# Half of an expert piece loaded ahead, bias tables moved to SyncE's queue, and later waits on TensorE, in a three-layer transformer kernel

## The chip, the cores and the metric

One core of a Trainium2 chip runs the whole program. The metric is the device time of one execution in microseconds. Three executions of the kernel before are known, and one profiled execution with its trace.

## The reference, cut to what matters

256 tokens of width 1024 go through three layers, all in float32. Layers one and two each have a mixer and then a retrieval step (PEER): every token picks 128 rows out of a table of 16384 (8 heads, 16 picks each), takes the dot product of its activation with the first half of the row, and adds the second half weighted by it. The third layer has a mixer with three kinds of attention, whose bias tables come from two small parameter tensors, and a mixture of 32 experts.

```
act = gelu(einsum('td,thkd->thk', xb, u[ib])) * gb      # retrieval, 128 tokens at a time
y   = einsum('thk,thkd->td', act, v[ib])
...
logits = einsum('bhcd,bhacjd->bhcaj', q_r, k_win) * scale + bias   # last mixer, one of its parts
...
a = silu(xb @ w1[e]) * (xb @ w3[e])                       # expert
return a @ w2[e]
```

## The kernel before, in words

Each engine has its own program, written out by hand; they meet in semaphores. SyncE (SP) issues nearly all loads of weights, GpSimd (POOL) the gathers, and each queue issues in program order: a wait stands in the way of everything behind it.

**Retrieval.** `PICKS` = 512 gathers, numbered 0 to 511, make up four tiles of 128 (two layers by two tiles of tokens). A gather (L1036) brings one picked row for each of 128 tokens, 8 KB each, so 1 MiB, into one of `ROWS` = 8 buffers. VectorE takes the dot product (L3153), ScalarE makes a diagonal matrix of the weights (`weigh_row`, L2305, L2308, L2311), and TensorE adds the row into PSUM (`sum_row`, L1560). POOL issues gather n only when gather n-8 has been summed. Between the rows the engines do the mixer of the next layer in small steps, by a step number s that is written out: `second_layer(t)` on TensorE (L1708) and on ScalarE. At s = 5, 64 and 81 TensorE transposes a tile of activations (`turn_tile`, L1632), ScalarE copies it into `hT` (`move_turned_tile`, L2366, L2371), and TensorE waits for the copy in the same step (`d_hT`), though the first product that reads it comes at s = 9, 67 and 84. `rows_to` is called at the top of every step, so sums that are due stand between the steps. This happens for both values of t: six places in all.

**The last mixer.** Its weights come in 10 slots of 2 MiB through a ring of `RING` = 4 places in the first 64 KB of `arena`, which the row buffers have used until then. SP waits for gather 509 (L870, `near`), and then loads the first four (L873), each when the row buffers in its place are summed: the first two need the sums of gathers 505 and 507, the third that of gather 510, the fourth that of gather 511. The fifth and later slots are loaded when TensorE has finished with the slot that had the place (L808). The bias tables, `dil_bias` (one transfer of 2304 KB in runs of 1536 bytes, L1040) and `na_bias` (16 transfers of 96 KB in runs of 256 bytes, L1045), are loaded by POOL once the last rows have been added to `x`, and then the gain `g_ffn` (512 KB, L956). VectorE adds a mask to `na_bias` in `mask_tables` (L2763) after the first two head scalings; the first reader of the tables is `last_bias(0)` (L2736).

**The experts.** They run in `QUADS` = 8 groups of four; a group has `PIECES` = 12 pieces of 2 MiB: 0 to 7 for `up` (L1967), 8 to 11 for `down` (L2016). Of group 0 the first `AHEAD` = 11 pieces are loaded before the stage, 0 to 7 in the eight `moe_slot` places (the last two of which are outside the ring) and 8 to 10 in leftover strips of other buffers (`BITS`). From piece 11 on all pieces go through `MOE_RING` = 6 places. TensorE counts pieces it has finished in `p_used`; SP waits for it before each load (`next_piece`, L882). Piece 11 takes the place of piece 0, and pieces 0 to 4 of group 1 those of pieces 1 to 5 of group 0; piece 5 of group 1 takes the place of piece 11, so it is issued at `p_used` = 12, after the whole `down(0)`.

Before the experts a router picks them. TensorE works out the router's products (`route_tile`, L1182), VectorE the choice (L3462 to L3504), and meanwhile TensorE transposes the scaled second tile of `h` (`turn_scaled`, L1201), ScalarE copies it to `hT` (`move_half`, L2472), and TensorE runs products whose results nobody reads (`keep_clock`, L1128). `hT` is read in the experts' stage only by a branch for experts with more than 32 tokens (L2044), which runs over all experts again when its flag is set.

Of the kernel before, what the change touches and what calls it, by code (L numbers as in the profile page):

```python
# [240 lines left out]
def program(nc, a, out):  # L241
    ctx = ExitStack()
    with ctx:
# [483 lines left out]

        def down_piece(q, n):
# [71 lines left out]
        def _(sync):  # L800
# [68 lines left out]
            near = PICKS - 3  # L869
            sync.wait_ge(row_in[near % ROWS], landed(near))  # L870
            for n in range(phase_slots["in2"][0], phase_slots["in2"][0] + RING):
                sync.wait_ge(vsum, rows_left(place[n]))
                sync.dma_start(ring[:, place[n], :], a["w_slots"][n]).then_inc(w_landed[place[n]], 16)  # L873
            for n in range(phase_slots["in2"][0] + RING, len(slots)):
# [28 lines left out]
            sync.wait_ge(r_mm, T)  # L903
            sync.wait_ge(y_ready, 3)
# [39 lines left out]
        def _(pool):  # L944
# [74 lines left out]
            for n in range(PICKS):  # L1019
# [13 lines left out]
                else:  # L1033
# [5 lines left out]

            pool.dma_start(dil_bias, bass.AP(tensor=t5_rep.tensor, offset=127,  # L1040
                                             ap=[[12 * TW - 1, P], [TW, 12], [1, 384]])).then_inc(bias_in, 16)
            W = NA_HEADS * NDR * RW
            for hh in range(NA_HEADS):
                for r2 in range(2):
                    pool.dma_start(na_bias[r2 * GRID_W:(r2 + 1) * GRID_W, hh, :].rearrange("p (j n) -> p j n", j=6),  # L1045
                                   bass.AP(tensor=na_rep.tensor,
                                           offset=hh * NDR * RW + (1 - r2) * RW + GRID_W - 1,
                                           ap=[[W - 1, GRID_W], [RW, 6], [1, GRID_W]])).then_inc(bias_in, 16)
# [11 lines left out]
        def _(pe):  # L1060
# [135 lines left out]
            def turn_scaled(b):  # L1196

                n = turned[0]
                for c in range(4):
                    k = 4 * b + c  # L1200
                    mm = pe.transpose(sp_[:, b, c * P:(c + 1) * P], h[:, 1, k * P:(k + 1) * P], ident)  # L1201
# [2471 lines left out]
```

## Time and profile before

| | us |
|---|---|
| median of 3 executions | 2306.08 (2305.84 to 2307.43) |
| the profiled execution | 2306.09 |
| its span in the trace | 2304.3 |
| TensorE busy | 1789.9 (78%) |
| VectorE busy | 1298.3 (56%) |
| ScalarE busy | 850.6 (37%) |
| GpSimd busy | 659.1 (29%) |
| moved by DMA | 920.49 MB, 399 GB/s over the span |

Times in the trace count from the span's start. A busy share is an average over stages with different limits; what bounds a stage is read in the stage.

### The profile page before, as it was taken

The numbers are of one execution on the slowest core, as the hardware profiler recorded it, in microseconds if no ns is written. First come the engines' busy times: TensorE is split into PE (matmuls) and PEld (weight loads), VectorE is DVE, ScalarE is ACT, GpSimd is POOL, SyncE is SP. The second block draws the span as 40 slices with busy tenths as digits, with TensorE's granted clock in tenths as the row PEclk, the third lists the DMA queues.
The fourth block names the chain that finished last, engine by engine and source line by source line (L and its number), as shares of the span: only waits on it lengthen the run. The fifth ranks groups of instructions, "written<-read, shape, count | busy, mean of one in ns | idle before, by whom it ended". The sixth has DMA issues, their size and how long they took to land.

```text
span 2304.3 us, 30881 instructions
## 1 busy us (share of the span) xinstructions
PE 1789.9 (78%) x11196; PEld 848.4 (37%) x11196; DVE 1298.3 (56%) x3217; ACT 850.6 (37%) x2292; POOL 659.1 (29%) x606
## 2 busy tenths in 40 slices
PE   9999877695797777588779666877779997766666
PEld 4655521161352343153336112343327553222222
DVE  4878887668757766866776867555442331111111
ACT  1324354444445544454744435444333520000000
POOL 1002444434433433533443444333322300000000
PEclk9999887696798888689989667888979999788888
DMA  9988799999999999999999999999999399999998
GB/s 395 381 351 347 314 420 421 420 420 419 388 421 421 421 421 421 421 382 421 412 410 421 421 420 421 421 421 420 421 404 333 121 392 422 428 428 429 428 428 372
DMA packets 111150, 920.49 MB, mean 399 GB/s; under 512 B 12806, under 2 KB 15140, under 8 KB 19044
## 3 DMA queue, kind: packets, MB, share of 16 engines
q0 software_dynamic: 76800, 549.70, 57.9%
q1 hardware_dynamic: 34212, 369.02, 38.8%
q8 instruction: 78, 1.28, 0.2%
q14 instruction: 60, 0.49, 0.1%
HBM read 917.57 MB, written 6.06 MB: 401 GB/s over the span
## 4 chain that ended last, share of the span: by engine, by line
DMA 48%; PE 32%; DVE 10%; ACT 6%; issue 3%; POOL 1%; SPq 0%; DVEq 0%; POOLq 0%; ACTq 0%
DMA arena<-in_peer_uv_dram,arena 27%; DMA arena<-in_moe_pieces_dram 14%; PE summed L1560 8%; DVE y_g L3153 4%; PE gp L1652 3%; PE gp L1105 3%; DMA mod<-in_w_parts_dram 3%; DMA arena<-in_w_slots_dram 2%; PE gp L1967 2%; PE gp L1110 2%; PE gp L1648 2%; DMA arena<-in_w_parts_dram 1%; PE gp L1781 1%; ACT arena L2311 1%; PE gp L1532 1%
## 5 line engine op out<-in xcount | busy, mean ns | idle before, releaser
L1560 PE MATMUL summed<-arena 64*64 64x512 f32 x4096 | 693.8, 773 | 338.5 <-ACT arena L2311 313.9
L3153 DVE CUSTOM_DVE_ANT_0 y_g<-arena,h 128x1024 f32<-128x1024 f32 x512 | 627.3, 1225 | 389.6 <-DMA arena<-in_peer_uv_dram,arena 332.1
L1036 POOL DMA_INDIRECT arena<-in_peer_uv_dram,arena x512 | 592.8, 1158 | 885.9 <-PE summed L1560 805.4
L1560 PEld LDWEIGHTS summed<-arena 64*64 64x64 f32 x4096 | 136.3, 157 | 760.3 <-ACT arena L2311 660.3
L2305 ACT ACTIVATE arena<-arena 128x1 f32<-128x1 f32 x512 | 102.7, 201 | 558.0 <-DVE arena L3153 556.9
L1967 PE MATMUL gp<-arena,mod 128*32 128x512 f32 x1008 | 156.5, 758 | 98.5 <-DMA arena<-in_moe_pieces_dram 98.5
L2311 ACT ACTIVATE arena<-cst,arena 128x128 f32<-128x128 f32 x512 | 205.5, 401 | 16.8
L3546 DVE TENSOR_TENSOR mod<-mod,gp 128x512 f32<-128x512 f32 x8 | 5.5, 687 | 353.7 <-ACT mod L2620 353.7
L2308 ACT ACTIVATE arena<-arena 128x1 f32<-128x1 f32 x512 | 150.8, 294 | 16.6
L1967 PEld LDWEIGHTS gp<-arena,mod 128*32 128x32 f32 x1008 | 31.7, 124 | 214.8 <-DMA arena<-in_moe_pieces_dram 156.8
L2620 ACT ACTIVATE mod<-gp 128x512 f32<-128x512 f32 x8 | 4.8, 597 | 246.7 <-PE gp L1967 246.7
L1105 PE MATMUL gp<-arena,hT 128*128 128x512 f32 x208 | 92.8, 603 | 1.0 <-DMA arena<-in_w_slots_dram 0.5
L2884 DVE SCALAR_TENSOR_TENSOR h<-arena,cst,h 128x512 f32<-128x512 f32 x98 | 73.9, 754 | 3.4
L2305 ACT ACT_TABLE_LOAD x54 | 69.3, 1283 | 0.9
L1942 PE MATMUL summed<-mod,h 128*128 128x128 f32 x256 | 46.8, 368 | 22.5 <-DVE mod L3541 22.4
L3065 DVE FIND_INDEX8 arena<-arena 128x8 uint32<-128x128 f32 (+1 forms) x192 | 61.7, 329 | 0.0
L3062 DVE MAX8 arena<-arena 128x8 f32<-128x128 f32 (+1 forms) x192 | 58.4, 332 | 5.6 <-ACT arena L2280 2.2
L1105 PEld LDWEIGHTS gp<-arena,hT 128*128 128x128 f32 x208 | 39.5, 194 | 52.5 <-issue 50.1
L2093 ACT ACTIVATE arena<-gp 128x512 f32<-128x512 f32 (+1 forms) x26 | 15.3, 589 | 113.6 <-PE gp L1119 40.3
L1119 PE MATMUL gp<-hT,arena 128*128 128x256 f32 x256 | 56.3, 381 | 0.7 <-ACT hT L2105 0.7
L2016 PE MATMUL scores<-arena,mod 128*32 128x256 f32 x952 | 54.3, 380 | 0.7 <-ACT mod L2624 0.7
L1942 PEld LDWEIGHTS summed<-mod,h 128*128 128x128 f32 x256 | 45.3, 279 | 25.0 <-DVE mod L3541 24.0
(530 smaller groups left out, 2339.3 us busy)
## 6 DMA issues: line engine op xcount, KB each, us to landing
arena<-in_moe_pieces_dram SPq DMA_DIRECT2D x92, 2048.0 KB, 25.5
arena<-in_w_slots_dram SPq DMA_DIRECT2D x43, 2048.0 KB, 12.5
arena<-in_w_parts_dram SPq DMA_DIRECT2D x42, 1024.0 KB, 9.3
mod<-in_w_parts_dram SPq DMA_DIRECT2D x23, 1024.0 KB, 9.6
arena<-in_peer_uv_dram,arena POOLq DMA_INDIRECT x512, 15.7
t_rep<-t_rows POOLq DMA_DIRECT2D x1, 3066.0 KB, 18.3
arena<-t_rep POOLq DMA_DIRECT2D x1, 2304.0 KB, 12.8
ext<-in_w_parts_dram SPq DMA_DIRECT2D x2, 1024.0 KB, 22.8
```

Source lines behind the costliest of these rows:

```text
L1036: pool.indirect_dma_start(rowbuf[b], None, a["peer_uv"].rearrange("l n d -> (l n) d"), bass.IndirectOffsetOnAxis(ap=idx[:, col(n):col(n) + ...
L1105: mm = pe.matmul(bank, hT[:, k, grp[1] * P:(grp[1] + 1) * P], w[:, k, :], start=k == 0, stop=k == KT - 1)
L1560: mm = pe.matmul(op[o:o + HALF, b, :], diag[i:i + HALF, n % DIAGS, i:i + HALF], rowbuf[n % ROWS][i:i + HALF, D + b * 512:D + (b + 1) * 512 ...
L1652: mm = pe.matmul(bank[:, c * P:(c + 1) * P], w[k][:, c * P:(c + 1) * P], hT[:, k, tok], start=k == 0, stop=k == KT - 1)
L1942: mm = pe.matmul(op[:, k // 4, (k % 4) * P:(k % 4 + 1) * P], h[:, t, k * P:(k + 1) * P], sel[:, t, :], start=t == 0, stop=t == T - 1)
L1967: mm = pe.matmul(gp[c, j, :], xe[:, 2 * kk + k, c], w[:, e, k, :], start=kk + k == 0, stop=kk == 3 and k == 1, skip_group_check=True)
L2305: link(act.activation(coef[:, c:c + 1], dots[:, c:c + 1], ACT.Gelu))
L2308: link(act.activation(coef[:, c:c + 1], coef[:, c:c + 1], ACT.Copy, scale=gate[:, c:c + 1]))
L2311: act.activation(diag[:, n % DIAGS, :], ident, ACT.Copy, scale=coef[:, c:c + 1]).then_inc(diag_ready, 1)
L2884: ins = v.scalar_tensor_tensor(out=acc, in0=w[:, k, :], scalar=cact[:, k:k + 1], in1=acc, op0=ALU.mult, op1=ALU.add)
L3065: ins = v.max_index(w[:, part], b[:, part], s)
L3153: v.tensor_tensor_reduce(y[:, t, :], rowbuf[n % ROWS][:, 0:D], h[:, t, :], 1.0, 0.0, ALU.mult, ALU.add, dots[:, c:c + 1]).then_inc(udot, 1)
```

## The change

1. TensorE's waits for `d_hT` after `turn_tile` move from the steps s = 5, 64 and 81 to 9, 67 and 84 (both t).
2. The bias tables are loaded by SP, behind the last mixer's first four weight slots and ahead of its fifth, on the semaphore `loaded`. The wait for `bias_w` and for the two halves of `x` comes with them. POOL goes from the last gather to the gain and `divide_last`.
3. Of the first four slots only the first is still issued behind gather 509; the second waits for gather 511 to land.
4. `mask_tables` comes first in VectorE's `last_attention`.
5. A square root on one column (`small[:, 16:17]`, written by ScalarE and read by nobody) is inserted behind the last row on ScalarE.
6. `turn_scaled` and `move_half` of the router's stage move into the rarely taken branch, there for both tiles. So `hT` is free from the router's products on.
7. The first half of piece 11 of group 0 (1 MiB) is loaded into `hT`, behind the router's products (`r_mm`) and ahead of the last two strips of pieces 9 and 10. At `p_used` = 1 only the second half is left to load, into the ring's place. The strips' semaphore counts one more transfer, and TensorE waits for it before it reads piece 11.

```diff
@@ down_piece
+            if isinstance(q, int) and q == 0 and n == AHEAD:
+                split = [flat_hT[:, c:c + S] for c in range(0, 8 * S, S)]
+                split += [moe_slot[piece_place(q, n)][:, c:c + S] for c in range(8 * S, 16 * S, S)]
+                return lambda e, f: split[4 * e + f]
@@ piece_landed
-                return 16 if n not in BITS else 16 * sum(len(bits) for bits in BITS.values())
+                return 16 if n not in BITS else 16 * (1 + sum(len(bits) for bits in BITS.values()))
@@ SyncE
-            near = PICKS - 3
-            sync.wait_ge(row_in[near % ROWS], landed(near))
             for n in range(phase_slots["in2"][0], phase_slots["in2"][0] + RING):
+                if n < phase_slots["in2"][0] + 2:
+                    near = PICKS - 3 if n == phase_slots["in2"][0] else PICKS - 1
+                    sync.wait_ge(row_in[near % ROWS], landed(near))
                 sync.wait_ge(vsum, rows_left(place[n]))
                 sync.dma_start(ring[:, place[n], :], a["w_slots"][n]).then_inc(w_landed[place[n]], 16)
+            sync.wait_ge(bias_w, 64)
+            sync.wait_ge(x_ready, 4 * T + 1)
+            sync.dma_start(dil_bias, bass.AP(...)).then_inc(loaded, 16)
+            for hh in range(NA_HEADS):
+                for r2 in range(2):
+                    sync.dma_start(na_bias[...], bass.AP(...)).then_inc(loaded, 16)
...
             sync.wait_ge(r_mm, T)
+            sync.dma_start(flat_hT, a["moe_pieces"][0, AHEAD][:, 0:8 * S]).then_inc(p_in[AHEAD - 1], 16)
             sync.wait_ge(y_ready, 3)
             sync.wait_ge(h_ready, 5 * T + 5)
             first_bits(9, (1, 2))
             first_bits(10, (1, 2))
             for n in range(AHEAD, PIECES):
                 sync.wait_ge(p_used, n - AHEAD + 1)
-                next_piece(0, n)
+                r = piece_place(0, n)
+                sync.dma_start(moe_slot[r][:, 8 * S:], a["moe_pieces"][0, n][:, 8 * S:]).then_inc(p_in[r], 16)
@@ GpSimd
-            pool.dma_start(dil_bias, ...).then_inc(bias_in, 16)
-            for hh in range(NA_HEADS):
-                for r2 in range(2):
-                    pool.dma_start(na_bias[...], ...).then_inc(bias_in, 16)
@@ TensorE, second_layer (the same at s == 64 / 67 and 81 / 84)
                     if s == 5:
                         pe.wait_ge(d_h, 2 * t + 1)
                         turn_tile(h, t)
+                    if s == 9:
                         pe.wait_ge(d_hT, 6 * t + 2)
@@ TensorE, router
             pe.wait_ge(h_ready, 5 * T + 7)
-            turn_scaled(0)
-            turn_scaled(1)
             keep_clock("out2", 2, h[:, 0, 0:CH])
@@ TensorE, down
                     pe.wait_ge(p_in[r], piece_landed(p, 8 + b))
+                    if first(p) and 8 + b == AHEAD:
+                        pe.wait_ge(p_in[AHEAD - 1], piece_landed(p, AHEAD - 1))
@@ TensorE and ScalarE, in the branch on the flag
+                for t in range(T):
+                    for b in range(2):
+                        turn_scaled(t, b)      # ScalarE: move_half(b, (gp, sp_)[t][:, b, :], t)
@@ ScalarE
             rows_to(PICKS)
+            act.activation(small[:, 16:17], eps[:, 0:1], ACT.Sqrt)
             half_square(1, 0, x_ready, 4 * T)
...
-            act.wait_ge(r_mm, T)
-            for b in range(2):
-                move_half(b, sp_[:, b, :])
@@ VectorE
-                v.wait_ge(bias_in, 16 * (NA_HEADS + 17))
+                v.wait_ge(loaded, 16 * (NLOADS + 20))
...
             def last_attention():
+                mask_tables()
                 head_inverse("block2", 0)
                 head_scale("block2", 0)
                 head_scale("block2", 1)
                 head_inverse("block2", 1)
-                mask_tables()
```

## Rows read from the trace of the kernel before

**Rows 1.** The page: rates in 40 slices, and the chain that ended last, by engine.
```profile
GB/s 395 381 351 347 314 420 421 420 420 419 388 421 421 421 421 421 421 382 421 412 410 421 421 420 421 421 421 420 421 404 333 121 392 422 428 428 429 428 428 372
DMA 48%; PE 32%; DVE 10%; ACT 6%; issue 3%; POOL 1%; SPq 0%; DVEq 0%; POOLq 0%; ACTq 0%
```

**Rows 2.** Busy time by stretch: stretch, length, engines, granted clock, DMA share, GB/s.
```profile
615.00:619.00 4.00, 4.00 (x32) 1.08 (x24) 2.99 (x9) 2.31 (x8) 2.23 (x2) 0.70 0.37 111
640.00:960.00 320.00, 244.89 (x1545) 116.43 (x1547) 225.81 (x571) 158.01 (x441) 130.82 (x108) 0.84 1.01 421
991.00:995.00 4.00, 4.00 (x24) 1.24 (x20) 2.77 (x9) 2.50 (x10) 2.19 (x2) 0.50 0.51 166
1167.00:1170.00 3.00, 3.00 (x22) 1.96 (x15) 2.75 (x7) 0.85 (x3) 2.39 (x3) 1.00 0.79 265
```

**Rows 3.** Timeline of TensorE: start, duration, engine, line, work, [idle before <- releaser].
```profile
609.91 1.97 PE L1632 MATMUL turned<-cst,h 128*128 128x128 f32 x8
614.01 5.32 PE L1560 MATMUL summed<-arena 64*64 64x512 f32 x32 [2.13 <-ACT hT L2371]
990.22 6.65 PE L1560 MATMUL summed<-arena 64*64 64x512 f32 x32 [2.14 <-ACT hT L2371]
1163.50 4.49 PE L1560 MATMUL summed<-arena 64*64 64x512 f32 x24 [1.43 <-ACT hT L2366]
```

**Rows 4.** Timeline of GpSimd, the gather behind the first of these places.
```profile
616.29 1.48 POOL L1036 DMA_INDIRECT arena<-in_peer_uv_dram,arena  x1 [4.94 <-PE summed L1560]
```

**Rows 5.** Timeline of ScalarE at the same place.
```profile
609.76 0.40 ACT L2311 ACTIVATE arena<-cst,arena 128x128 f32<-128x128 f32 x1
611.06 2.90 ACT L2371 ACTIVATE hT<-turned,cst 128x128 f32<-128x128 f32 x8 [0.89 <-PE turned L1632]
```

**Rows 6.** Timeline at the last gathers: SyncE's issues, and VectorE's last two rows.
```profile
1701.77 0.81 SPq L873 DMA_DIRECT2D arena<-in_w_slots_dram  x2
1704.24 1.23 DVE L3153 CUSTOM_DVE_ANT_0 y_g<-arena,h 128x1024 f32<-128x1024 f32 x1 [1.23 <-DMA arena<-in_peer_uv_dram,arena]
1709.16 1.23 DVE L3153 CUSTOM_DVE_ANT_0 y_g<-arena,h 128x1024 f32<-128x1024 f32 x1 [3.69 <-DMA arena<-in_peer_uv_dram,arena]
```

**Rows 7.** The last mixer's start: timelines, line L1045, and a stretch with tables.
```profile
1713.36 8.67 PE L1105 MATMUL gp<-arena,hT 128*128 128x512 f32 x16
1717.70 1.28 ACT L2479 ACT_TABLE_LOAD   x1
1731.14 0.33 SPq L808 DMA_DIRECT2D arena<-in_w_slots_dram  x1
1738.00:1740.00 2.00, 2.00 (x21) 2.00 (x20) 0.00 (x0) 1.32 (x3) 0.00 (x0) 1.00 0.94 198
1745.90 2.28 PE L1110 MATMUL gp<-hT,arena 128*128 128x128 f32 x18
L1045 POOL DMA_DIRECT2D mod<-na_rep x16: 662/669/745, 1718.6 to 1757.2; - x16
1766.53 3.84 DVE L2763 TENSOR_TENSOR mod<-mod,cst 128x384 f32<-128x384 f32 x8 [2.33 <-DMA mod<-na_rep]
```

**Rows 8.** Timeline of the router's stage, TensorE and VectorE.
```profile
1863.22 1.96 PE L1201 MATMUL scores<-cst,h 128*128 128x128 f32 x8
1867.09 0.29 DVE L3496 TENSOR_TENSOR arena<-arena 128x32 f32<-128x32 f32 x2
1867.54 0.31 PE L1927 MATMUL turned<-arena,mod 128*128 128x32 f32 x2
```

**Rows 9.** The experts' start: SyncE's issues before and after its long wait; DMA there.
```profile
1875.24 2.04 SPq L882 DMA_DIRECT2D arena<-in_moe_pieces_dram  x2
1883.83 0.33 SPq L882 DMA_DIRECT2D arena<-in_moe_pieces_dram  x1
1905.47 0.33 SPq L882 DMA_DIRECT2D arena<-in_moe_pieces_dram  x1
1905.00:1908.00 3.00, 3.00 (x36) 1.04 (x32) 0.00 (x0) 1.02 (x1) 0.00 (x0) 1.00 0.89 300
```

More of the change, by code:

```diff
@@ L726, in program @@
         moe_slot = [ring[:, place[n], :] for n in last_held] + [zbuf[:, 0:4096], tk[:, 0:4096], arena[:, 28672:32768], y_g2[:, :]]
+        flat_hT = hT[:, :, :].rearrange("p k n -> p (k n)")
         def down_piece(q, n):
@@ L867, in _ @@
                 sync.dma_start(ring2[q % 2], a["w_parts"][WQ1 + PARTS + 2 + i]).then_inc(w1_in[q % 2], 16)
-            near = PICKS - 3
-            sync.wait_ge(row_in[near % ROWS], landed(near))
             for n in range(phase_slots["in2"][0], phase_slots["in2"][0] + RING):
+                if n < phase_slots["in2"][0] + 2:
+                    near = PICKS - 3 if n == phase_slots["in2"][0] else PICKS - 1
+                    sync.wait_ge(row_in[near % ROWS], landed(near))
                 sync.wait_ge(vsum, rows_left(place[n]))
                 sync.dma_start(ring[:, place[n], :], a["w_slots"][n]).then_inc(w_landed[place[n]], 16)
+            sync.wait_ge(bias_w, 64)
+            sync.wait_ge(x_ready, 4 * T + 1)
+            sync.dma_start(dil_bias, bass.AP(tensor=t5_rep.tensor, offset=127,
+                                             ap=[[12 * TW - 1, P], [TW, 12], [1, 384]])).then_inc(loaded, 16)
+            W = NA_HEADS * NDR * RW
+            for hh in range(NA_HEADS):
+                for r2 in range(2):
+                    sync.dma_start(na_bias[r2 * GRID_W:(r2 + 1) * GRID_W, hh, :].rearrange("p (j n) -> p j n", j=6),
+                                   bass.AP(tensor=na_rep.tensor,
+                                           offset=hh * NDR * RW + (1 - r2) * RW + GRID_W - 1,
+                                           ap=[[W - 1, GRID_W], [RW, 6], [1, GRID_W]])).then_inc(loaded, 16)
             for n in range(phase_slots["in2"][0] + RING, len(slots)):
@@ L1038, in _ @@
             pool.wait_ge(x_ready, 4 * T + 1)
-            pool.dma_start(dil_bias, bass.AP(tensor=t5_rep.tensor, offset=127,
-                                             ap=[[12 * TW - 1, P], [TW, 12], [1, 384]])).then_inc(bias_in, 16)
-            W = NA_HEADS * NDR * RW
-            for hh in range(NA_HEADS):
-                for r2 in range(2):
[L1045 to L1048, printed above, removed]
             load_gain(5, a["g_ffn_2"][0])
@@ L1194, in turn_plain, with turn_scaled @@
                 turned[0] += 1
-            def turn_scaled(b):
+            def turn_scaled(t, b):
                 n = turned[0]
@@ L1738, in second_layer @@
                         turn_tile(y, t)
+                    if s == 67:
                         pe.wait_ge(d_hT, 6 * t + 4)
@@ L1744, in second_layer @@
                         turn_tile(h, t)
+                    if s == 84:
                         pe.wait_ge(d_hT, 6 * t + 6)
@@ L2467, in half_square, with move_half @@
                                accum_out=small[:, 46 + b:47 + b]).then_inc(sumsq, 1)
-            def move_half(b, bank):
+            def move_half(b, bank, t=1):
                 act.wait_ge(turn_done, turned[0] + 1)
-                act.activation(hT[:, 4 * b:4 * b + 4, P:S], bank.rearrange("p (c n) -> p c n", c=4), ACT.Copy).then_inc(turn_moved, 1)
+                act.activation(hT[:, 4 * b:4 * b + 4, t * P:(t + 1) * P], bank.rearrange("p (c n) -> p c n", c=4), ACT.Copy).then_inc(turn_moved, 1)
                 turned[0] += 1
@@ L2657, in _ @@
             with act.If(act.value_load(flag[0:1, 0:1], min_val=0, max_val=2 * S) > 0):
+                for t in range(T):
+                    for b in range(2):
+                        move_half(b, (gp, sp_)[t][:, b, :], t)
                 expert(0, 0)
```

2 lines of the change are left out of this document (1 added, 1 removed).

## The prediction, made before the changed kernel was run

> **What bounds the kernel now.** I read the page's rates first [rows 1]. From slice 6 on most slices stand at 420 to 429 GB/s, and a slice is 57.6 us. The retrieval steps (about 240 to 1710 us) and the experts (from about 1875 us) are bound by transfers. The chain of waits gives DMA 48% and TensorE 32%; TensorE's share lies mostly in the last mixer, the slices at 333 and 121 GB/s, where its products run back to back.
>
> The next view is the busy time by stretch. The long stretch 640 to 960 us shows the full rate, 421 GB/s at a DMA share of 1.01 [rows 2]. A change inside a stretch like that gains nothing by freeing an engine. So I looked for places where the rate falls, and found three short ones: 615 to 619 us at 111 GB/s, 991 to 995 at 166, 1167 to 1170 at 265 [rows 2]. Against 421 they lose 4 x (1 - 111/421) = 2.9 us, 2.4 us and 1.1 us.
>
> **The waits on TensorE (part 1).** TensorE's timeline shows what comes before each dip [rows 3]. At 609.91 it transposes for 1.97 us, then stands idle for 2.13 us until ScalarE's copy L2371 ends, and only then sums at 614.01. Yet ScalarE had finished the diagonals of the two gathers that were due by 610.16, before its 2.90 us of copies began [rows 5]. POOL waits for these sums before it issues the next gather, which comes at 616.29 after 4.94 us of waiting [rows 4]. From 615 on there is nothing in flight. The second place is the same with 2.14 us of idle time, the third has 1.43 us [rows 3].
>
> With the wait moved to the step that reads `hT`, the sums start 2.13 us sooner, the two later ones of the four are ready by then, and step 9 finds the copy long done. Gather 140 is issued 2.1 us sooner. The dip is longer than that (2.9 us), so the whole 2.1 us comes back, and the stage runs at full rate afterwards, which keeps it. The terms are 2.1 us, 2.1 us (dip 2.4), and 1.1 us at the third, where the dip is shorter than the stall. At the other three of the six places the rate never falls, so there the gain is nothing: those rows are covered by gathers in flight. Sum: **-5.3 us**. Bounds: nothing, if TensorE's later steps take it up; the three dips together, 6.4 us.
>
> **The second weight slot held back (part 3).** The last two gathers were taken up at 1704.24 and 1709.16, 4.92 us apart [rows 6], where full rate gives 1 MiB in 2.49 us. So the weight slots issued at 1701.77 cost the last gather some 2.4 us. The change leaves the first slot where it is and takes away only the second. The first alone holds 2 MiB, 4.98 us of all engines, and until 1709 that much more than covers what was mixed in. I take **0**: the last gather still has a weight transfer beside it to the end. The bound on the other side is the whole 2.4 us. The Trainium skill, "DMA: Bandwidth & Descriptors", section "Queues, rings and completion order", says that each DMA engine takes turns between queues packet by packet. By that rule one slot in SP's queue costs the gather as much as two, which agrees with my 0; sharing by transfers in flight would give back a third of the 2.4 us, 0.8 us.
>
> **The square root ahead (part 5).** It takes the table load of 1.28 us at 1717.70 off the path of the norm. But TensorE's L1105 runs from 1713.36 to 1722.03 and must end before the next step [rows 7], so this gains **0**; if L1105 did not cover it, 1.28 us.
>
> **The tables on SP's queue (parts 2 and 4).** On POOL the 16 transfers of `na_bias` were issued from 1718.6 to 1757.2, and the mask ran at 1766.53 in its place [rows 7]. TensorE was busy through all of that, so earlier tables give nothing. The cost is the fifth weight slot, now behind them in one queue. It was issued at 1731.14, and TensorE needs it at 1745.90 [rows 7]. I work out when it lands. The second slot is issued at 1709.2; with some 1.5 us until bytes flow (an estimate, from the dip that ends about that long after POOL's issue at 616.29), three slots of 4.90 us at the page's 428 GB/s end at 1725.4. `dil_bias` (2.36 MB) takes 5.5 us, the gain on POOL's queue, now earlier, 1.2 us. For `na_bias` (1.57 MB) the nearest row is the stretch 1738 to 1740, filled mostly with it, at 198 GB/s: 7.9 us. Then 4.9 us for the slot: 1744.9. That is 1.0 us before the need: **0**. By bytes alone it is 4.2 us earlier. The upper bound is POOL's own pace, 38.6/15 = 2.6 us for each table. Everything behind the waiting SP is this slot and the later ones, whose needs lie 7 us apart.
>
> A rule speaks against this part. The same page, section "Issuing engines are not separate DMA queues", says that starting transfers from several engines saves only time to issue them. By it the move costs no bandwidth and buys none.
>
> **The router's stage (part 6).** Eight transposes of 1.96 us go. The products behind them wait for VectorE's choice, which ends at 1867.38, and L1927 starts at 1867.54 [rows 8]. At most 0.1 us comes forward. ScalarE's two copies are beside the path too. I take **0**.
>
> **Half a piece ahead (part 7).** 1 MiB less in a stage bound by transfers looks like 2.45 us. But the ring is fed by TensorE here. SP issued the ring's first piece at 1875.24, its sixth at 1883.83 and nothing more until 1905.47, when `down(0)` was done and the place of piece 11 came free [rows 9]. In between the queue lived on six pieces, 6 x 4.90 = 29.4 us: with the 1.5 us to the first byte it was dry at 1906.1, and the next piece's bytes came at 1907.0. The stretch 1905 to 1908 agrees, 300 GB/s instead of 428, a loss of 0.9 us. With half a piece less it runs dry 2.4 us earlier, and piece 5 of group 1 is still issued when `down(0)` ends. The dip grows by what was saved. The half in `hT` and the strips behind it are needed only in `down(0)`, after `up(0)` and a gather, so their 2.4 us of delay is covered; without that cover it would be paid. So **0**; the other bound is 2.45 us.
>
> **Sum.** The profiled execution took 2306.09 us (span 2304.3 and 1.8 around it), within 0.01 of the median. 2306.1 - 5.3 = **2300.8 us**, span 2299.0. Some 0.2%, 4.6 us, is about what a measurement of this kernel can tell from no change; the bounds are 2301.5 and 2310.7.
>
> **The rivals.**
> *A: the tables delay the fifth slot a little.* If a table takes 0.6 to 0.9 us on SP's queue instead of 0.49 (runs of 256 bytes; the stretch that I priced was not all tables), the slot lands up to 5.5 us late: 2301.5 to 2306. For it: the margin is only 1 us.
> *B: the earlier sums come to nothing.* TensorE has 32 products of L1652 per pair of rows after step 9; if these pace the stage, the gathers are still late afterwards and 1 to 3 us of the 5.3 remain: 2303 to 2305. Against it: TensorE's whole schedule moves by the same 2.1 us.
> *C: more than I allow.* The last gather lands on time (2.4), or the half piece pays (2.45), the reading that a transfer-bound stage pays by bytes: about 2298.4, or 2296 with both. Against it: rows 6 and 9.
> *D, slower: the tables hold SP.* If SP is held for each table as POOL was, 2.6 us each, it reaches the fifth slot at 1718 + 17 x 2.6 = 1762, which lands about 6.4 us later, 22 us after the need: 2323. It decides from 0.49 + 6.3/16 = 0.88 us per table on, where margin (1.0) and gain (5.3) are used up; at 1.2 us it is slower by over 0.2%. Against it: POOL's pace is that of its issues, while the stretch above shows tables moving five times as fast.
> *E: the change does not do what it says*: the half piece ahead is such a part, and it is in the forecast.
>
> **How the numbers follow.** Forecast 0.52 (its own range 2299.3 to 2302.3, a fifth of it above 2301.5), A 0.20, B 0.12, C 0.10, D 0.06. Faster by over 0.2%: 0.42 of the forecast and all of C, 0.52. Slower: D and what lies beyond A, 0.07. Within: 0.41. The range runs from 2298.0, in the middle of C, to 2306.5, the end of A; it leaves out D and half of C.
>
> **What would show it.** Right: no idle time of TensorE on L2371 or L2366 before L1560; 615 to 619 near full rate, and everything behind it 2 us earlier; the last gather still some 4.9 us after the one before; TensorE never idle on the fifth slot; a deeper dip ahead of the issue at `p_used` = 12. Wrong: dips that stay though the waits are gone (B), TensorE waiting for a weight slot near 1745 (A or D), or a stage from 1905 on that is shorter than before (C).

## The result: slower by 0.35%, and the profile after

| | us |
|---|---|
| kernel before, median of 7 runs | 2307.1 (2305.8 to 2310.8) |
| changed kernel, median of 7 runs | 2314.84 (2312.95 to 2316.85) |
| ratio, 95% interval | 1.0035 (1.0025 to 1.0045) |
| profiled execution, span | 2312.7 (before 2304.3) |

I had forecast 2300.8 us. The changed kernel is about 8 us slower than the one before, outside my range. The spans of the two profiled executions differ by 8.4 us. First the stretches of [rows 2] again, in the changed kernel: stretch, length, engines, granted clock, DMA share, GB/s.

```profile
615.00:619.00 4.00, 3.19 (x27) 1.74 (x28) 2.67 (x10) 3.17 (x11) 2.73 (x2) 1.00 1.02 401
640.00:960.00 320.00, 245.98 (x1534) 115.30 (x1526) 225.97 (x570) 158.10 (x441) 137.59 (x108) 0.83 1.01 420
991.00:995.00 4.00, 4.00 (x37) 1.97 (x30) 2.56 (x10) 2.96 (x11) 3.08 (x4) 1.00 0.83 297
1167.00:1170.00 3.00, 3.00 (x15) 2.64 (x15) 2.86 (x8) 1.72 (x6) 1.77 (x2) 1.00 0.96 355
```

The dips filled, the first wholly and the other two in large part: 401 GB/s instead of 111, 297 instead of 166, 355 instead of 265. But the stage did not get shorter. VectorE's sum over a tile's rows (L3172, now L3189), the last step of a tile, starts at 597.05 before and 597.98 after for the first tile, and at 1713.50 and 1714.49 for the last. That is 1116.45 us in one and 1116.51 in the other. The 0.9 us at 597 lies ahead of all that was changed there.

Then the last mixer. The timelines of SyncE's queue and TensorE, and two stretches (lines moved: L808 is now L814, L1110 is L1121). The last two rows are the same stretches in the kernel before:

```profile
1718.40 25.29 SPq L889 DMA_DIRECT2D mod<-na_rep  x16
1743.73 32.81 SPq L814 DMA_DIRECT2D arena<-in_w_slots_dram  x6
1751.62 16.18 PE L1121 MATMUL gp<-hT,arena 128*128 128x128 f32 x128 [4.48 <-DMA arena<-in_w_slots_dram]
1734.00:1738.00 4.00, 4.00 (x38) 4.00 (x37) 0.00 (x0) 0.00 (x0) 0.00 (x0) 1.00 1.02 178
1738.00:1742.00 4.00, 4.00 (x38) 4.00 (x38) 0.00 (x0) 1.32 (x3) 0.00 (x0) 1.00 0.75 140
```
```profile
1734.00:1738.00 4.00, 4.00 (x39) 4.00 (x38) 0.00 (x0) 0.00 (x0) 2.53 (x4) 1.00 1.01 404
1738.00:1742.00 4.00, 4.00 (x39) 4.00 (x37) 0.00 (x0) 1.32 (x3) 0.00 (x0) 1.00 1.02 260
```

SyncE needs 25.29 us to hand over 16 tables. It issues the fifth weight slot at 1743.73 instead of 1731.14 [rows 7], and TensorE stands idle for 4.48 us until it has landed. The products behind the wait, 128 of them, take 16.18 us, at a granted clock of 0.58 from 1751.6 to 1754; in executions without a wait they take 14.56. From the start of L1105 to the start of VectorE's choice (L3496) the stretch has grown from 153.73 to 160.09 us: **+6.4**.

And the router's stage, TensorE's timeline and its granted clock:

```profile
1874.79 0.61 PE L1939 MATMUL turned<-arena,mod 128*128 128x32 f32 x2 [2.24 <-DVE arena L3513]
1874.00:1876.00 2.00, 1.21 (x6) 1.21 (x7) 1.23 (x9) 0.00 (x0) 0.00 (x0) 0.71 1.02 438
1876.00:1878.00 2.00, 2.00 (x5) 0.92 (x5) 1.49 (x7) 0.00 (x0) 0.00 (x0) 0.50 1.00 422
1878.00:1880.00 2.00, 2.00 (x11) 2.00 (x10) 1.79 (x8) 0.00 (x0) 0.00 (x0) 0.50 0.91 385
```

TensorE has nothing to do for 2.24 us, and behind the choice its granted clock is 0.5 (1.2 GHz): the work that took 0.31 us in [rows 8] takes 0.61 now. From the choice to the start of `down(0)` it is 33.12 us instead of 31.20: **+1.9**. From there to the end it is 405.1 instead of 406.0: **-0.9**. With the 1.0 us that was there at L1105 (0.9 of it at 597) this adds up to 8.4.

### The profile page after: what moved, and what is told of

It is laid out like the page before. It is cut to its first block, busy times and chain, and to the rows that moved or that the text cites. A ratio compares the mean times of both kernels' runs of the same rounds, so it can differ in the third digit from the quotient of the medians.

```text
span 2312.7 us, 30863 instructions
## 1 busy us (share of the span) xinstructions
PE 1788.8 (77%) x11188; PEld 848.1 (37%) x11188; DVE 1297.3 (56%) x3217; ACT 851.2 (37%) x2291; POOL 652.9 (28%) x589
## 4 chain that ended last, share of the span: by engine, by line
DMA 46%; PE 34%; DVE 9%; ACT 6%; issue 3%; SPq 1%; POOL 1%; DVEq 0%; POOLq 0%; ACTq 0%
DMA arena<-in_peer_uv_dram,arena 26%; DMA arena<-in_moe_pieces_dram 14%; PE summed L1571 8%; DVE y_g L3170 4%; PE gp L1663 3%; PE gp L1116 3%; PE gp L1130 2%; PE gp L1979 2%; DMA arena<-in_w_parts_dram 2%; DMA mod<-in_w_parts_dram 2%; PE gp L1795 1%; PE gp L1659 1%; ACT arena L2328 1%; SPq L889 1%; PE gp L1543 1%
## 5 line engine op out<-in xcount | busy, mean ns | idle before, releaser
L1979 PEld LDWEIGHTS gp<-arena,mod 128*32 128x32 f32 x1008 | 31.6, 124 | 215.5 <-DMA arena<-in_moe_pieces_dram 157.7
L1954 PEld LDWEIGHTS summed<-mod,h 128*128 128x128 f32 x256 | 45.2, 278 | 25.2 <-DVE mod L3558 24.1
```

The costliest lines, as they stand in the source:

```text
L1954: mm = pe.matmul(op[:, k // 4, (k % 4) * P:(k % 4 + 1) * P], h[:, t, k * P:(k + 1) * P], sel[:, t, :], start=t == 0, stop=t == T - 1)
L1979: mm = pe.matmul(gp[c, j, :], xe[:, 2 * kk + k, c], w[:, e, k, :], start=kk + k == 0, stop=kk == 3 and k == 1, skip_group_check=True)
```

## Experiments

Every kernel was timed against the one before on the same chip. Their intervals are 2 to 4 us to each side, so for single microseconds I read the traces. Four stretches serve for that, each from start to start: the stage of the rows (first to last L3172), the mixer (L1105 to L3496), from there to `down(0)` (L2016), and the rest. Of each kernel there is one profiled execution, which need not lie at the median.

### Each part alone

`waits_only` is the kernel before with part 1:

```
                         turn_tile(h, t)
+                    if s == 9:
                         pe.wait_ge(d_hT, 6 * t + 2)
```

> The kernel before with part 1 alone (the waits for the copies of hT moved to the steps that read it). The forecast's theory: the 2.1, 2.1 and 1.1 us that TensorE stood still are gained, 5.3 us. The rival, from the trace of the changed kernel (its third tile of gathered rows ends 0.99 us later than before, as its first tile did already, whose code is the same): the time is given back further on in the same stage, where stretches of 420 us and more a slice now stand lower: 0, within 1 us. In both the idle time of TensorE on L2371 is gone and 615 to 619 us stands near 400 GB/s; what differs is the end of the last tile of rows, about 1708 or about 1713.5.

Measured: 0.9991 (0.9981 to 1.0002). The stretch 615 to 619 stood at 395 GB/s, and 619 to 623, where the same work lies in this execution, which is 4.3 us later at the first tile, at 389. The stage took 1116.95 us. The forecast's 5.3 us are not there.

`tables_sp` has parts 2 and 4, `dil_bias` and the 16 tables moved from POOL's program to SP's:

```
+                    sync.dma_start(na_bias[r2 * GRID_W:(r2 + 1) * GRID_W, hh, :]..., ...).then_inc(loaded, 16)
...
+                mask_tables()
                 head_inverse("block2", 0)
```

> The kernel before with parts 2 and 4 alone (the bias tables on SyncE's queue, their mask earlier; the second weight slot is not held back). Theory T: a table costs 0.65 us on SP's queue, 16 of them 10.4 us, dil_bias 6.4, and the fifth weight slot lands behind them. The queue is not dry for 2.5 us as it was in the changed kernel at 1708 to 1711, so the slot lands about 2.5 us earlier than its 1751.6 less 1: near 1748, 2 us after the need of 1745.9, and TensorE's clock, which fell after the wait, costs up to 1.7 us more: +2 to +4 us. The forecast's theory: 0, TensorE never waits for the fifth slot. Rival: the cost in the changed kernel came from the tables alone, slot held back or not: +6.4 us.

Measured: 1.0024 (1.0015 to 1.0033), +5.5 us. Its mixer took 159.48 us instead of 153.73, +5.75.

```profile
1717.07 24.71 SPq L882 DMA_DIRECT2D mod<-na_rep  x16
1741.82 32.79 SPq L808 DMA_DIRECT2D arena<-in_w_slots_dram  x6
1749.68 16.18 PE L1112 MATMUL gp<-hT,arena 128*128 128x128 f32 x128 [4.26 <-DMA arena<-in_w_slots_dram]
```

So the tables alone make most of the loss, and more than the +2 to +4 that I expected, although the queue was not dry here.

`router_only` has part 6:

```
             pe.wait_ge(h_ready, 5 * T + 7)
-            turn_scaled(0)
-            turn_scaled(1)
             keep_clock("out2", 2, h[:, 0, 0:CH])
```

> The kernel before with part 6 alone (the eight transposes of h and the two copies of hT's second half are done only in the branch that hardly runs). Theory C: with the transposes gone TensorE runs out of work some 2 us before VectorE's choice is there, its granted clock falls to 0.5, and what stands behind it takes 3 us longer, of which 1 us is given back in the gathers: +2 us, with the granted clock at 0.5 to 0.7 in the 4 us behind the choice. The forecast's theory: 0. Rival: the 2 us of the changed kernel came from the half piece and the strips behind it; then this is 0 though the clock falls.

Measured: 1.0000 (0.9989 to 1.0011). Choice to `down(0)`: 31.26 us, as before. Here the clock fell too, but from 1866 to 1870, under the filling products ahead of the choice, and had come back (0.96 in 1870 to 1872). The loss is thus not part 6 as such. It comes when the low clock falls behind the choice.

That happens without part 6 too. In `tables_half` and `dil_on_sp` (both below), which keep the transposes, TensorE stood idle for 1.40 us ahead of the choice's result, and then its clock was low. Both rows are from `tables_half`:

```profile
1870.86 0.41 PE L1937 MATMUL turned<-arena,mod 128*128 128x32 f32 x2 [1.40 <-DVE arena L3507]
1872.00:1874.00 2.00, 2.00 (x6) 1.07 (x5) 1.86 (x9) 0.00 (x0) 0.00 (x0) 0.50 0.95 404
```

Over all sixteen profiled kernels: where TensorE idled 2.2 us there, the clock was low behind the choice in four of four; where it idled 1.4 us, in two of eight; where it idled 0.5 us or not at all, in none of four. In the kernel before, the clock was low ahead of the choice (0.58 from 1865 to 1867), which stretched the products until the choice was there. In the six executions with the low clock behind it the stretch from the choice to `down(0)` took 32.4 to 33.1 us, in the ten others 30.0 to 31.6. `tables_half` and `dil_on_sp`, at 32.65 and 32.87 us, have neither part 6 nor the half piece, so the growth needs neither.

`all_but_tables` is the changed kernel without parts 2 and 4:

> The changed kernel with parts 2 and 4 undone (the tables back on POOL's queue, their mask in its old place). Theory T: the 6.4 us that the stretch from the last gathered row to the end of the fifth slot's groups grew by are gone: about 2308.4 us, +1 to +2 against the kernel before. Rival: the slot held back is what makes the fifth slot late; then TensorE still waits for it near 1746 us, and 3 to 4 us remain there: 2311 to 2312.

Measured: 1.0001 (0.9991 to 1.0011). The mixer took 154.31 us and TensorE did not wait for the fifth slot. Its clock was low behind the choice, and from there to `down(0)` it took 32.95 us. What is left of the change is worth nothing, in sum.

### What about the tables costs

`tables_slot_held` adds part 3 to `tables_sp`:

```
+                if n < phase_slots["in2"][0] + 2:
+                    near = PICKS - 3 if n == phase_slots["in2"][0] else PICKS - 1
+                    sync.wait_ge(row_in[near % ROWS], landed(near))
```

> The kernel before with parts 2, 3 and 4 (tables on SyncE's queue and the second weight slot held back until the last gathered row has landed). Theory T+G: the tables cost the 5.5 us of the run with them alone; the slot held back leaves the queues dry near 1708 to 1711 us, 2.3 us of transfers that then lie ahead of the tables and the fifth slot, which TensorE gets near 1751.5 us: +7.5 to +8 us against the kernel before, +2.3 against the run with the tables alone. Rival: held back or not, the fifth slot is late by the tables only: +5.5. The forecast's theory: 0.

Measured: 1.0037 (1.0024 to 1.0051). The time fits either theory, the trace (of the fastest of its five executions, 2311.87 us) doesn't: the transfers did run thin, 238 GB/s at 1710 to 1714, but the mixer took 159.64 us, TensorE waited 3.97 us, and SyncE was through with the tables at 1742.99, 28.6 us after the start of L1105, just as in `tables_sp` (28.8). The slot held back costs nothing that shows beside the tables, and the +2.3 us that I had expected for it is not there: SyncE sets the time of the fifth slot, not the bytes ahead of it.

`tables_half` leaves 8 of the 16 tables on POOL's queue:

```
             for hh in range(NA_HEADS):
-                for r2 in range(2):
+                for r2 in range(1):
                     sync.dma_start(na_bias[r2 * GRID_W:(r2 + 1) * GRID_W, hh, :]...
```

> The kernel before with dil_bias and only 8 of the 16 tables on SP's queue; the other 8 stay on POOL's, and the mask stays in its old place. Theory T (a price for each table, 0.65 us on SP's queue): 8 x 0.65 = 5.2 us less ahead of the fifth slot, which in the run with all 16 held TensorE up for 4.26 us: no wait, 0 against the kernel before, within 1 us. Rival Q: what makes the slot late is its place behind three slots and dil_bias in one queue, the tables for POOL take the same bytes from the same engines: TensorE still waits 2 to 3 us for the fifth slot, +3 us or more.

Measured: 1.0037 (1.0023 to 1.0051). The profiled execution is the fastest of its five, 2311.0 us against a median of 2314.25; what the other four lost beyond it no trace shows.

```profile
1717.92 23.26 SPq L882 DMA_DIRECT2D mod<-na_rep  x8
1741.23 31.40 SPq L808 DMA_DIRECT2D arena<-in_w_slots_dram  x6
1749.33 14.56 PE L1120 MATMUL gp<-hT,arena 128*128 128x128 f32 x128 [2.27 <-DMA arena<-in_w_slots_dram]
```

Half the tables hold SyncE for 23.26 us instead of 24.71. So the time is not one price times the number of tables, and theory T, which had no wait here, falls. The single issues say more. With all 16 tables, in the changed kernel, the first lasted 9.69 us, the next five 1.5 to 2.0 us each, and the last ten 0.63 us each, one of them 0.93. With 8 the first lasted 10.86 us and the fourth 4.12. The longest and the shortest stand in the view of the line (shortest/median/longest, in ns), here the changed kernel and then `tables_half`:

```profile
L889 SPq DMA_DIRECT2D mod<-na_rep x16: 626/634/9687, 1718.4 to 1742.8; - x16
L882 SPq DMA_DIRECT2D mod<-na_rep x8: 625/1564/10862, 1717.9 to 1740.6; - x8
```

I read this as SyncE standing in the first issues while the weight slots and `dil_bias` ahead are moved; only the last ten of 16 go at the 0.65 us that theory T gave to all.

`dil_on_sp` leaves all 16 tables on POOL's queue and moves `dil_bias` alone:

```
+            sync.dma_start(dil_bias, ...).then_inc(loaded, 16)
...
-            pool.dma_start(dil_bias, ...).then_inc(bias_in, 16)
```

> The kernel before with dil_bias alone on SP's queue; all 16 tables of na_bias stay on POOL's, and the mask stays in its place. Idle time of TensorE on the fifth weight slot was 4.26 us with 16 tables on SP's queue and 2.27 us with 8. Theory P (each table on SP's queue costs the slot 0.25 us and more, as small packets that the same copy on POOL's queue does not have): with none of them the line through both ends at 0.3 us: no wait or a trace of one, 0 against the kernel before, and up to 1 us faster where POOL's tables, now started earlier, spare VectorE its wait ahead of the mask. Rival Q (being ahead of the slot in time is what counts, whatever queue it comes by): TensorE still waits 2 us or more for the slot, +2 us or more.

Measured: 1.0009 (1.0001 to 1.0018), about +2 us. That is what rival Q had, but not for its reason: SyncE issued the fifth slot at 1732.83, when its place came free, and TensorE did not wait for it. The mixer took 154.93 us, 1.2 more than before, and 1.7 us more went by behind the choice, at the low clock. POOL issued its last table at 1763.58 (before 1757.2, in an execution that was 1.8 us earlier at L1105), VectorE waited 5.29 us ahead of the mask, and TensorE 1.21 us behind that:

```profile
1771.17 3.84 DVE L2767 TENSOR_TENSOR mod<-mod,cst 128x384 f32<-128x384 f32 x8 [5.29 <-DMA mod<-na_rep]
1775.97 1.14 PE L1259 MATMUL scores<-arena 64*128 64x256 f32 x8 [1.21 <-DVE arena L2727]
```

This wait is there in the kernel before too [rows 7, the last]; in its profiled execution TensorE's other work covered it.

Two kernels then held another engine, or held SyncE one slot later. `tables_half_scalar` issues the 8 tables of `tables_half` on ScalarE's own queue, ahead of `last_projection()` in its program:

```
             move_turned_rows(1)
+            for hh in range(NA_HEADS):
+                act.dma_start(na_bias[0:GRID_W, hh, :]..., ...).then_inc(loaded, 16)
             last_projection()
```

> As the run with 8 tables and dil_bias on SP's queue, with these 8 tables on ScalarE's queue instead, issued in its gap behind the copies of hT (1723.6 to 1731.1). Theory H (SyncE is held: in the run with 8 tables it reached the fifth slot at 1741.2 instead of 1731.1, and TensorE waited 2.27 us): SyncE issues the slot as in the kernel before, within 1 us of the place being free, and TensorE does not wait for it; 0 to +1 us against the kernel before, from the small packets and from VectorE's wait ahead of the mask. Rival Z (the small packets' engine time ahead of the slot is what counts): TensorE still waits 1.5 to 2.5 us for the slot though it was issued in time. A third outcome, that ScalarE is held by its own queue past 1731, would show as TensorE idle on ScalarE's copy of the first groups.

Measured: 1.0051 (1.0034 to 1.0067), +11.8 us, and it is the third outcome. Timelines of ScalarE's queue, ScalarE, SyncE's queue and TensorE:

```profile
1724.44 23.45 ACTq L2585 DMA_DIRECT2D mod<-na_rep  x7
1747.93 0.60 ACT L2096 ACTIVATE arena<-gp 128x512 f32<-128x512 f32 x1 [23.50 <-issue]
1731.92 50.83 SPq L808 DMA_DIRECT2D arena<-in_w_slots_dram  x6
1748.67 10.28 PE L1113 MATMUL gp<-hT,arena 128*128 128x128 f32 x64 [9.64 <-ACT arena L2096]
```

SyncE is free and issues the slot in time (the 50.83 us are six slots with waits between). ScalarE is held instead, for 24.1 us by 8 tables, with nothing ahead of them in its own queue. What moved in 1715 to 1765 us, in this kernel and in the one before (queue, kind: packets, MB, share of the 16 engines):

```profile
q1 hardware_dynamic: 2228, 12.35, 69.9%
q10 hardware_dynamic: 3200, 0.79, 9.5%
q0 software_dynamic: 528, 1.31, 8.8%
```
```profile
q1 hardware_dynamic: 864, 12.57, 68.9%
q0 software_dynamic: 1295, 3.93, 27.4%
```

In q10 are the 8 tables, 0.79 MB in 3200 packets, 400 for a table of 96 KB. In the kernel before all 16 tables and `dil_bias`, 3.93 MB, went in 1295 packets of POOL's queue. An estimate from the shares: q10 used 9.5% of 50 us, 4.75 us, 0.6 us of engine time for a table; yet the 8 took five times as long, beside `dil_bias` and weight slots in SyncE's queue (q1). The first three issues on ScalarE took 0.64 to 0.69 us each, the seventh 10.83. The Trainium skill, "DMA: Bandwidth & Descriptors", section "Queues, rings and completion order", says that a DMA engine changes between queues after a packet; small packets that take turns with large ones would be held up like this. The trace agrees with that: from 1729 to 1746 us q1 moved 1447 packets and q10 1709, near to one for one, but 4.86 MB and 0.42 MB. No run here took the large ones away.

`slot_then_tables` issues the fifth slot first, and then `dil_bias` and all 16 tables:

```
+            load_weights(phase_slots["in2"][0] + RING)
             sync.wait_ge(bias_w, 64)
```

> As the run with all tables on SP's queue, with the fifth weight slot issued ahead of dil_bias and the 16 tables. SyncE waits for the slot's place until 1731 us and only then hands the tables over. Theory H: the fifth slot is on time, and the hold moves to the sixth, which is issued after 1731 + 0.4 + 16 x 0.63 = 1741.5 at the earliest, up to 1750 if the ring holds SyncE as it did; it lands 7 to 8 us later, against a need at 1753.2: a wait of 0 to 4 us, and the mask, whose tables now land near 1750, is not late. Against the kernel before: 0 to +4 us, and less than the +5.5 us of the run with the tables first. Rival Z: the same bytes and packets lie ahead of the sixth slot, +4 to +6 us.

Measured: 1.0046 (1.0030 to 1.0062), +10.6 us.

```profile
1730.16 20.56 SPq L883 DMA_DIRECT2D mod<-na_rep  x16
1750.77 26.07 SPq L808 DMA_DIRECT2D arena<-in_w_slots_dram  x5
1759.29 8.80 PE L1113 MATMUL gp<-hT,arena 128*128 128x128 f32 x64 [7.80 <-DMA arena<-in_w_slots_dram]
```

The hold moves with the tables, and the sixth slot pays. The time lies beyond both forecasts, H's 0 to +4 us and Z's +4 to +6; what speaks for H is that the sixth slot was late in its issue. I had allowed an issue by 1750; it came at 1750.77 and the slot landed 8.5 us later. The need was at 1751.5, not 1753.2, as this execution reached L1105 1.6 us earlier. Theory H names the mechanism, my price was too low.

### Where the 5.3 us went

`transposes_doubled` does the opposite of part 1, each transpose at the six places twice:

```
-                    for c in range(4):
+                    for c in range(8):
+                        c = c % 4
```

> The kernel before with each transpose at the six places of part 1 done twice, so that TensorE and the copies behind it are 2 us later at each, the opposite of part 1. The forecast's theory (a dip of the transfers at three of the six places costs the stage what TensorE is late): the stage from the end of the first tile of rows (597.05) to the end of the last (1713.50), 1116.4 us, grows by 2 us at each of the three dips or more, +6 us. Rival B (the stage has slack elsewhere that takes up what is won or lost at these places): it grows by 0 to 2 us.

Measured: 1.0001 (0.9985 to 1.0017). The sums behind the first place began 5.23 us after the start of the transposes, against 4.10 in [rows 3]. That is 1.1 us more, not 2, as the wait for ScalarE's copy became shorter, 1.59 us instead of 2.13. At the other two dips it is 0.9 and 1.0 us, so the forecast's theory would give +3 us here and not +6. The stage took 1116.27 us. Over all profiled kernels it took 1116.16 us on average in the five with part 1 (1115.41 to 1116.95) and 1116.5 in the ten that have neither part 1 nor the doubled transposes (1114.91 to 1118.13): a difference of 0.4, inside the spread of either. So the stage takes up what is won or lost at these places.

Two things can be ahead, and they part here: the transfers and the rows. On average over the five kernels with part 1 and the ten without, each counted from the end of its first tile, the gathers 140 to 168 (615 to 701 us) are issued 1.8 to 2.6 us sooner, and the bytes moved are ahead by 2.3 us of full rate. But gathers 172 to 198 (712 to 787 us) are issued only 0.4 us sooner, and VectorE takes up its rows only 0.2 us sooner (rows 140 to 171) and then 0.5 us (rows 172 to 198). The second tile ends 376.09 us after the first instead of 376.40, the third 752.82 instead of 753.25. Behind the second dip it is the same: gathers 272 to 296 are issued about 3 us sooner, gather 300 (1089 us) 0.1. In the kernel before and in `waits_and_dil` (below), which has part 1, the second and third tile end at:

```profile
973.25 0.68 DVE L3172 TENSOR_TENSOR y_g<-y_g,summed 128x512 f32<-128x512 f32 x1
1350.27 0.68 DVE L3172 TENSOR_TENSOR y_g<-y_g,summed 128x512 f32<-128x512 f32 x1
```
```profile
973.76 0.68 DVE L3179 TENSOR_TENSOR y_g<-y_g,summed 128x512 f32<-128x512 f32 x1
1350.69 0.68 DVE L3179 TENSOR_TENSOR y_g<-y_g,summed 128x512 f32<-128x512 f32 x1
```

The first tile ended at 597.05 and 597.61. So hardly any of the first 2.1 us ever reached VectorE's rows, and the gathers had lost most of it by 712 us. Which engine held them back is not shown.

The lead of the transfers lasts longer, and the trace shows where it goes. It is the stretch 1110 to 1160 us, in which VectorE has both the dot products and the attention's work. The kernel before, then `waits_and_dil`: the stretch, and all that VectorE waited for in it (waited for: us in total, times, longest):

```profile
1110.00:1160.00 50.00, 36.20 (x255) 15.48 (x253) 42.80 (x100) 35.81 (x96) 22.62 (x19) 0.90 1.01 412
DVE h L3218 <- PE scores L1679: 2.1, 1, 2.1
DVE arena L3218 <- PE scores L1679: 1.3, 1, 1.3
DVE den L3230 <- PE gp L1704: 1.3, 1, 1.3
DVE small L3274 <- ACT small L2447: 0.2, 1, 0.2
```
```profile
1110.00:1160.00 50.00, 36.16 (x252) 15.34 (x252) 42.73 (x101) 35.82 (x96) 22.25 (x19) 0.89 0.98 377
DVE h L3225 <- PE scores L1682: 2.2, 1, 2.2
DVE arena L3225 <- PE scores L1682: 1.3, 1, 1.3
DVE den L3237 <- PE gp L1707: 1.3, 1, 1.3
DVE small L3281 <- ACT small L2453: 0.2, 1, 0.2
```

VectorE does the same 42.8 us of work and waits for no gathered row, in either. The engines set the pace here, and rows that came earlier only thin the transfers out: 377 GB/s instead of 412, which over 50 us is 50 x (412 - 377)/421 = 4.2 us of transfers, an estimate (the busy share of the DMA engines fell less, from 1.01 to 0.98). In the five kernels with part 1 the rate was 377 to 393 here, 385 on average, in the ten without it 395 to 420, 408 on average: 50 x (408 - 385)/421 = 2.7 us. A second place is 760 to 780 us, 388 to 419 GB/s with part 1 and 412 to 421 without. I did not try a kernel that makes VectorE faster in these stretches, so where the lead goes is read from the traces, not shown by a run.

### The half piece, and the clock

`router_half_piece` has parts 6 and 7, `router_half_piece_clock` has three more filling products ahead of the choice:

```
-            keep_clock("out2", 2, h[:, 0, 0:CH])
+            keep_clock("out2", 5, h[:, 0, 0:CH])
```

> The kernel before with parts 6 and 7 (transposes only in the branch, half of piece 11 ahead into hT). In the changed kernel the stretch from VectorE's choice to down(0) grew by 1.9 us and what is behind down(0) shrank by 0.9. Theory R (the ring is pinned by down(0)): the half piece alone brings nothing before down(0) and its strips cost nothing; all of the growth is TensorE's clock at 0.5 behind the choice. So: about +1 us where the clock falls there, 0 or -0.5 where it doesn't. Rival S: the strips behind the half piece are late for down(0) or share the queues with the first gathers: +1 to +2 us in this stretch at full clock too.

> As the run before it, with five instead of two filling products ahead of the choice, so that TensorE has work until the choice is there (the three added take up to 3 us at full clock, 5 us at half). Theory R: the clock stays at 1.00 or has come back by the choice, the stretch from the choice to down(0) is 31.3 us as in the kernel before, and what is behind it is 0.5 to 0.9 us shorter: -0.5 to -1 us. Rival S: still 32 to 33 us. Should the added products run past the choice, they hold the rank's products up by 1 to 2 us, which the timeline would show.

Measured: 0.9996 (0.9987 to 1.0005) and 1.0007 (0.9997 to 1.0017). Choice to `down(0)` took 32.76 us in the first, where the clock was 0.50 in 1870 to 1872, and 31.57 in the second, where it stayed at 1.00. So theory R holds there: the growth is the clock, 1.2 us of it. But the -0.5 to -1 us that I had forecast for the second is not there. The added products ran past the choice by some 0.2 us, and the profiled execution had a wait of 3.75 us of TensorE behind the mask, whose tables were late on POOL's queue; whether the other executions lost the gain in the same way no trace shows. Behind `down(0)` the five kernels with the half piece took 405.8 us on average (405.1 to 406.4), the eleven others, the one before among them, 406.3 (405.7 to 407.8): by these averages, whose ranges overlap, the half piece is worth some 0.5 us, not its 2.45.

### Candidates

`waits_and_dil` has part 1 and `dil_bias` on SP's queue, `waits_dil_half_piece` parts 6 and 7 as well:

> A candidate for the best version: the kernel before with part 1 and with dil_bias alone on SP's queue. The sum of the two runs with each alone: part 1 gave a ratio of 0.9991, dil_bias 0 to -1 us by theory P: 2304 to 2307 us, -1 to -3 against the kernel before. By rival Q of the first run here: +0 to +2.

> The run before it with parts 6 and 7 as well, which alone gave a ratio of 0.9996: behind down(0) 0.6 to 0.9 us shorter, ahead of it up to 1.6 us longer where TensorE's clock falls behind the choice. Against the run before it: -0.5 to +1 us. If the half piece paid by its bytes (2.45 us), it would be 2 us faster.

Measured: 1.0004 (0.9995 to 1.0012) and 1.0006 (0.9997 to 1.0014). TensorE waited 0.19 and 0.27 us for the fifth slot and about 1.5 us behind the mask. Neither is faster than the kernel before, and no version here is faster by more than the measurement can tell.

## Why the prediction was wrong

**The waits (part 1): the step "the whole 2.1 us comes back, and the stage runs at full rate afterwards, which keeps it" failed.** The dips were read right, and filled. But I took a gather issued sooner for a row taken up sooner. VectorE took up the rows behind the first dip 0.2 to 0.5 us sooner, not 2.1, and by the end of the second tile 0.3 us were left, although the rate in 640 to 960 was full before and after. What the transfers were still ahead went in 1110 to 1160, where the engines set the pace. Rival B came true whole, not in part; whether by the products of TensorE that it names is open. Measured: 0.4 us of the 5.3.

**The tables (part 2): the step "7.9 us" for `na_bias` failed, and the bound that I had set aside was nearly right.** I priced the tables by bytes from a stretch in which they moved on POOL's queue. On SP's queue the same bytes are far more packets, and they hold the engine that issues them. SyncE reached the slot at 1743.73; my rival D, with SyncE held for each table, had 1762, and the measured 25.29/16 = 1.58 us a table put into its working (1718 + 17 x 1.58) gives 1744.9. It was slower by over 0.2% from 1.2 us on, as D says, and I gave that 0.06. D's point was right and its reason off: it is not a price for each table, as 8 tables held SyncE for 23.26 us; the first six of the 16 took 18.3 of the 25.29 us. My argument against it, that the tables "moving five times as fast" on POOL's queue excludes a hold, took one queue's transfer rate for another queue's issue. The rule of the Trainium skill ("DMA: Bandwidth & Descriptors", "Issuing engines are not separate DMA queues") that I had set against this part would, as I read it, have the move cost no bandwidth; the measurement differs, 178 and 140 GB/s in 1734 to 1742 us where the kernel before had 404 and 260. The cost is 4.48 us of waiting, and 1.6 us of lower clock behind it, which I had left out.

**Right.** The second slot held back brought nothing: the last row was taken up 5.07 us after the one before (1705.08 and 1710.15), against 4.92 in [rows 6]. One slot beside the gather cost as much as two, which agrees with the rule of the Trainium skill that I cited there. That the square root ahead gives 0 was not tried alone; in the changed kernel the norm's first scaling starts 4.73 us after the tile's sum instead of 6.02, but the transposes behind L1105 start 8.69 us after its start, not sooner than the 8.51 before. The half piece: some 0.5 us, and the deeper dip came, 251 GB/s at 1915 to 1918.

**The router's stage (part 6): 0 was half right.** Alone it cost nothing. In four of the six kernels that have it, the changed one among them, the clock was low behind the choice, which in `router_half_piece` took 1.2 us; but so it was in two of the ten that don't have it. The term that I put at nothing is the idle time ahead of the choice: 2.2 us without the transposes and 1.4 with them, at full clock. That part 6 made the low clock come in the changed kernel is likely by these counts, and not shown.

## What to carry to other kernels

Before a transfer is moved to another engine's queue, look at its contiguous runs and at what is queued behind it: a copy in runs of 256 bytes can be cheap on GpSimd's queue and hold SyncE or ScalarE for 20 us and more, and what stands behind it in that program pays. A dip in the rate is worth its length only if the engine that takes up the rows gets ahead by it too: follow that engine's own times to the ends of the tiles, and not the rate alone. And work that seems beside the path may be what holds TensorE's clock through a wait: compare several traces before a low clock is put down to one edit.

## What was not expected of the hardware

- The same 16 tables: 400 packets each on a hardware queue (3200 for 8 tables), while 16 of them and `dil_bias` are 1295 on POOL's. In the whole execution the change took 1296 packets from POOL's queue and added 8096 to SP's, for the same 3.93 MB; 144 of the 8096 come with the piece that is loaded in two parts, as `router_half_piece` has them too (page, before and then after):

```profile
q0 software_dynamic: 76800, 549.70, 57.9%
q1 hardware_dynamic: 34212, 369.02, 38.8%
```
```profile
q0 software_dynamic: 75504, 545.77, 57.2%
q1 hardware_dynamic: 42308, 372.95, 39.3%
```

- Handing over 8 or 16 such tables takes an engine about as long (23.26 and 24.71 us on SyncE, 24.1 on ScalarE for 8). A table alone takes 0.63 us where nothing holds it up, and single issues lasted up to 10.9 us.
- POOL hands over tables five at a time, with 5 to 15 us between the fives. Where all 16 come that way the mask is late, by different amounts: VectorE waited from 2.3 us (the kernel before) to 7.8 us ahead of it, and TensorE behind it from nothing to 3.75 us.
